# Bidirectional RWKV-7 flow step: the scans on 64-token blocks of two head pairs instead of 128-token chunks of one

## The reference

```python
def wkv_scan(s0, r, w, k, v, a, b, reverse):
    def step(S, inp):
        r_t, w_t, k_t, v_t, a_t, b_t = inp
        sa = jnp.einsum('bhvk,bhk->bhv', S, a_t)
        S = S * w_t[:, :, None, :] + sa[..., None] * b_t[:, :, None, :] + v_t[..., None] * k_t[:, :, None, :]
        return S, jnp.einsum('bhvk,bhk->bhv', S, r_t)
    s_final, y = lax.scan(step, s0.astype(jnp.float32), (...), reverse=reverse)
...
for d, (s0, reverse) in enumerate(((s0_f, False), (s0_b, True))):
    decay = jnp.exp(-jnp.exp(w_log.astype(jnp.float32)))
    y_d, s_d = wkv_scan(s0, r, decay, kd, v, -kk, kk * a, reverse)
wkv = ys[0] + ys[1]
mu = jnp.mean(wkv, axis=-1, keepdims=True)
var = jnp.mean(jnp.square(wkv - mu), axis=-1, keepdims=True)
ln = ((wkv - mu) * lax.rsqrt(var + LNX_EPS)).reshape(B, T, D_RWKV) * p['lnx_w'] + p['lnx_b']
x_a = (ln + (bonuses[0] + bonuses[1]).reshape(B, T, D_RWKV)).astype(xn.dtype) * g_out
```

## Time and profile before

| | us |
|---|---|
| median of 3 runs | 2689.25 (2687.86 to 2693.72) |
| span of the profiled execution | 2688.9 |
| dense stage, to 1008.5 us of the span | 1008.5 |
| scan stage, 1008.5 to 1625.5 | 617.0 |
| last stage, 1625.5 to the end | 1063.5 |
| TensorE busy over the whole span | 2568.6 (96%) |
| VectorE busy | 1872.8 (70%) |
| ScalarE, GpSimd busy | 1081.2 (40%), 1188.7 (44%) |

### The profile page before, as it was taken

The page is one execution under the profiler, slowest core; times in us unless marked ns, Lnnn a source line. Parts: engine busy times, 40 slices in busy tenths (PEclk is TensorE's granted clock), DMA queues, the critical chain, the costliest instruction groups (busy, mean ns, idle before and its releaser), DMA issues.

```text
span 2688.9 us, 67501 instructions
## 1 busy us (share of the span) xinstructions
PE 2568.6 (96%) x28608; PEld 2413.9 (90%) x28608; DVE 1872.8 (70%) x2978; ACT 1081.2 (40%) x1978; POOL 1188.7 (44%) x1154
## 2 busy tenths in 40 slices
PE   4899999999999998999999998999799999999998
PEld 3899999999999996777777777999799999999998
...
GB/s 325 106 102 118 140 71 186 113 111 140 80 175 123 101 203 116 131 133 149 142 155 139 145 162 181 133 179 98 61 63 86 81 101 63 87 82 100 63 79 71
DMA packets 282409, 329.10 MB, mean 122 GB/s; under 512 B 76288, under 2 KB 215936, under 8 KB 273536
## 3 DMA queue, kind: packets, MB, share of 16 engines
...
## 4 chain that ended last, share of the span: by engine, by line
PE 85%; DVE 8%; issue 2%; ACT 2%; DMA 2%; SPq 1%; POOL 0%; DVEq 0%; ACTq 0%; POOLq 0%
PE ser L972 18%; PE gbank L972 13%; PE inv L972 11%; PE bank L972 11%; PE gbank L1416 8%; PE inv L1416 8%; PE ser L1416 7%; PE bank L1416 7%; DVE a_sum L2323 1%; DMA ring<-in_wblocks 1%; PE inv L1174 1%; DVE a_sum L2327 1%; PE bank L1157 1%; DVE a_sum L2331 1%; DVE a_lo L2297 1%
## 5 line engine op out<-in xcount | busy, mean ns | idle before, releaser
L954 POOL TENSOR_TENSOR w_lo<-raw_w,w_hi 128x512 fp32r<-128x512 f32 x264 | 427.3, 1632 | 366.9 <-ACT w_hi L1756 366.9
L849 POOL TENSOR_TENSOR wsp<-ring,wsp 128x1024 fp32r<-128x1024 f32 x67 | 205.2, 3063 | 653.9 <-ACT wsp L1518 653.9
L1756 ACT ACTIVATE w_hi<-raw_w 128x512 fp32r<-128x512 f32 x264 | 165.2, 633 | 261.6 <-PE ser L1416 98.4
L972 PE MATMUL ser<-xn_hi,wsp 128*128 128x384 f32 x816 | 217.1, 339 | 6.0 <-POOL xn_lo L855 6.0
L1416 PE MATMUL gbank<-a_hi,w_hi 128*128 128x288 f32 x616 | 185.8, 302 | 30.8 <-POOL w_lo L954 14.6
L972 PE MATMUL gbank<-xn_hi,wsp 128*128 128x384 f32 x800 | 212.6, 339 | 0.3 <-issue 0.3
L972 PE MATMUL bank<-xn_hi,wsp 128*128 128x384 f32 x800 | 210.2, 337 | 0.5 <-issue 0.5
L972 PE MATMUL inv<-xn_hi,wsp 128*128 128x384 f32 x800 | 210.4, 338 | 0.0
L2126 DVE TENSOR_TENSOR gmat<-gbank,gmask 128x1024 f32<-128x1024 f32 x144 | 175.6, 1219 | 43.8 <-PE gbank L972 43.0
L1742 ACT ACTIVATE a_hi<-a_sum 128x1152 fp32r<-128x1152 f32 x88 | 103.0, 1172 | 224.5 <-DVE a_sum L2331 78.6
L972 PE MATMUL gbank<-ub 64*64 64x128 f32 (+1 forms) x3456 | 179.4, 310 | 9.0 <-DVE gmat L2126 7.6
...
## 6 DMA issues: line engine op xcount, KB each, us to landing
...
ub<-op_d SPq DMA_DIRECT2D x144, 256.0 KB, 2.8
...
```

The lines of the kernel that those rows point to most:

```text
L849: GT(wsp[s % 2][1][:], ring[(N_ADA_RING + s) % RING][:], wsp[s % 2][0][:].bitcast(F32), ALU.subtract).then_inc(S["wsplit_lo"], 1)
L954: GT(w_lo[n % 4][:], src, w_hi[n % 4][:].bitcast(F32), ALU.subtract).then_inc(S["wl_ok"], 1)
L972: return nc.tensor.matmul(out, lhsT, rhs, start=start, stop=stop)
L1756: A(w_hi[s][:], raw_of(op)[:, m, :].rearrange("p (k c) -> p k c", k=KH), ACT.Copy).then_inc(S["wh_ok"], 1)
```

## The change

A unit is now one block of 64 tokens of two head pairs (a group), both directions: 4 groups x 18 blocks = 72 units again. `LEVELS` goes from 6 to 5, so that the inverse ends at level 4 with two units in flight instead of three, and `last_blocks` on ACT is gone. `gmat` holds 64 columns per product instead of 128: half the elements. The 128 partitions of the token-side tensors, which were 128 tokens, are now 64 tokens of pair 0 and 64 tokens of pair 1. The second head's inverse, triangle and `ur` lie in the other partition half, which the index `b ^ h` says, so that the products of serial_ur, serial_u, serial_s and serial_y are 64*64 products. The state has one 64x64 tile per head pair, head and direction: 128x256 instead of two 128x64. It is now also carried over 18 blocks instead of 9 chunks. The loops of all engines are written in a new order (the lists below). DRAM scratch and loads follow the new tiling: one load of two units (7 DMAs) instead of 5 DMAs per unit; the `bk` planes are written in rows of 64 elements instead of 128. The dense stage scans 18 blocks of 64 tokens instead of 9 of 128. The finals stay one chunk of 128 tokens and one head pair: 18 per group, one per unit from block 10 of a group on, in the last group two per unit in units 64 to 71, with two left for the tail instead of five.

```diff
-LEVELS = 6
+LEVELS = 5
...
-UNITS = PAIRS * NC
-SETS = 5
-LOADS = 7
+
+GROUPS = PAIRS // 2
+UNITS = GROUPS * NB
+SETS = 4
+DOUBLES = 4
+PLACES = 2 * DOUBLES
 TOKS = 2
 LATE = LEVELS - FIRST
 FIN_ORDER = [3, 4, 2, 5, 1, 6, 0, 7, 8]
+FIN_FROM = 10
...
+        ar_d = scratch("ar_d", [GROUPS, 2, NC, P, 2, 2, C])
+        bk_d = scratch("bk_d", [GROUPS, 2, NB, P, 2, 2, HD])
+        v_d = scratch("v_d", [GROUPS, NC, P, 2, P])
...
+        def moving_of(v, d, b):
+
+            return ub[set_of(v)][:, d, b:4:2, tokens_of(d, v)]
+
+        def still_of(v, d, x):
+
+            return ub[set_of(v)][:, d, 4 + 2 * token_half(d, v) + x, :].rearrange("p (b t) -> p b t", b=2)
...
-            def start_inverse(v, part):
+            def start_inverse(v):
 
                 q, g = v % 3, gmat[v % SETS]
-                if part == 0:
-                    pool.wait_ge(S["gram_ok"], 2 * v + 2)
-                    for b in halves_of:
-                        ch.step(GT(ltc[q][b, :, :], g[b, 0, :, 0, b], g[b, 1, :, 0, b], ALU.add))
-                        ch.settle()
-                else:
-                    GT(lm[v % 2][part - 1][:], ltc[q][:], two(offm[:, part - 1, :]), ALU.mult).then_inc(S[f"lm{FIRST + part - 1}_ok"], 1)
+                pool.wait_ge(S["gram_ok"], 2 * v + 2)
+                ch.step(GT(ltc[q][:], g[:, 0, :, 0, :], g[:, 1, :, 0, :], ALU.add))
+                ch.settle()
+                for lev in range(FIRST, LEVELS):
+                    GT(lm[v % 2][lev - FIRST][:], ltc[q][:], two(offm[:, lev - FIRST, :]), ALU.mult).then_inc(S[f"lm{lev}_ok"], 1)
...
-                for n, b in enumerate(halves_of):
-                    for d in range(2):
-                        GT(tt[v % 2][b, d, :, b], xt[b, place_of(v), :, :], two(ttm[b, d, :]), ALU.mult).then_inc(S["tri_ok"], 1)
-                    pool.wait_ge(S["tri_ok"], 4 * v + 2 * n + 2)
+                pool.wait_ge(S["xt_ok"], sums(round_of(v)))
+                for d in range(2):
+                    GT(tt[v % 2][:, d, :, :], xt[:, place_of(v), :, :], two(ttm[:, d, :]), ALU.mult).then_inc(S["tri_ok"], 1)
...
+            def gram(v, d):
+
+                if d:
+                    pe.wait_ge(S["gram_ok"], 2 * v + 1)
+                else:
+                    pe.wait_ge(*loaded(v))
+                    if v:
+                        pe.wait_ge(S["gram_ok"], 2 * v)
+                for h in range(2):
+                    hs = halves_of[h]
+                    for b in range(2):
+                        mm(banks[h][halves_of[b ^ h], gram_at(d, 0, 1)], moving_of(v, d, b)[hs, 0, :], still_of(v, d, 0)[hs, b, :], True, True)
+                for h in range(2):
+                    hs = halves_of[h]
+                    for b in range(2):
+                        mm(banks[h][halves_of[b], gram_at(d, 1, 2)], still_of(v, d, 0)[hs, b, :], moving_of(v, d, b)[hs, 1, :], True, True)
+                for h in range(2):
+                    hs = halves_of[h]
+                    for b in range(2):
+                        ins = mm(banks[h][halves_of[b], gram_at(d, 2, 4)].rearrange("p (a t) -> p a t", a=2), still_of(v, d, 1)[hs, b, :], moving_of(v, d, b)[hs, :, :], True, True)
+                ins.then_inc(S["gram_full"], 1)
...
             def ur_state(u):
 
-                (p, j), q = divmod(u, NC), u % LOADS
-                serial_free(u)
-                if j < NC_LAT:
-                    pe.wait_ge(S["s_ok"], 2 * (NC_LAT * p + j + 1))
-                    for d in range(2):
-                        for h in range(2):
-                            hs = halves_of[h]
-                            for b in halves_of:
-                                mm(ser[b, h, d * HD:(d + 1) * HD], ub[q][hs, d, 0, b], state[d][j % 2][hs, :], d == 0, False)
-
-            def serial_ur(u):
-
-                j, q, g = u % NC, u % LOADS, gmat[u % SETS]
+                x = u % 2
                 for d in range(2):
                     for h in range(2):
-                        for b in halves_of:
-                            ins = mm(ser[b, h, d * HD:(d + 1) * HD], g[:, d, h, 2, b], vb[q][:, d, halves_of[h]], j == NC_LAT and d == 0, d == 1)
+                        hs = halves_of[h]
+                        for b in range(2):
+                            ins = mm(ser[halves_of[b ^ h], h, d * HD:(d + 1) * HD], moving_of(u, d, b)[hs, 0, :], state[x][hs, b, d, :], d == 0, False)
+                ins.then_inc(S["us_full"], 1)
+
+            def serial_ur(u):
+
+                q, g = set_of(u), gmat[u % SETS]
+                pe.wait_ge(S["us_full"], u + 1)
+                for d in range(2):
+                    for h in range(2):
+                        for b in range(2):
+                            bs = halves_of[b]
+                            ins = mm(ser[halves_of[b ^ h], h, d * HD:(d + 1) * HD], g[bs, d, h, 2, :], vb[q][bs, d, token_half(d, u), halves_of[h]], False, d == 1)
                 ins.then_inc(S["ur_full"], 1)
 
             def serial_u(u):
 
-                pe.wait_ge(S["tri_ok"], 4 * u + 4)
-                pe.wait_ge(S["tt_ok"], u + 1)
+                for x in finals(u - 1):
+                    pe.wait_ge(S["std_ok"], x[2] + 1)
+                pe.wait_ge(S["tri_ok"], 2 * u + 2)
                 pe.wait_ge(S["ur_ok"], u + 1)
                 for d in range(2):
                     for h in range(2):
-                        for b in halves_of:
-                            ins = mm(ser[b, 0, P + (2 * h + d) * HD:P + (2 * h + d + 1) * HD], tt[u % 2][:, d, h, b], ur[:, h, d, :], True, True)
+                        for b in range(2):
+                            xs = halves_of[b ^ h]
+                            ins = mm(ser[halves_of[b], h, P + d * HD:P + (d + 1) * HD], tt[u % 2][xs, d, h, :], ur[xs, h, d, :], True, True)
                 ins.then_inc(S["u_full"], 1)
 
             def y_at(j, d):
-                return slice((2 + y_place(d, j)) * P, (3 + y_place(d, j)) * P)
+                return slice(2 * P + y_place(d, j) * HD, 2 * P + (y_place(d, j) + 1) * HD)
 
             def y_state(u):
 
-                j, q = u % NC, u % LOADS
-                pe.wait_ge(S["ur_ok"], u + 1)
-                if j < NC_LAT:
-                    for d in range(2):
+                j, x = u % NB, u % 2
+                pe.wait_ge(S["xt_ok"], sums(round_of(u) + 1))
+                for d in range(2):
+                    for b in range(2):
                         for hs in halves_of:
-                            mm(ser[hs, 1, y_at(j, d)], state[d][j % 2][hs, :], ub[q][hs, d, 1, :], d == 0, False)
+                            ins = mm(inv[hs, b, y_at(j, d)], state[x][hs, b, d, :], moving_of(u, d, b)[hs, 1, :], d == 0, False)
+                ins.then_inc(S["ys_full"], 1)
...
-                    turn(s)
+            for s in range(-LATE - 1, UNITS):
+                m, j = divmod(s, NC)
+                inverses, serial, ahead = in_flight(s), there(s), there(s + 3)
+                if serial:
+                    serial_free(s)
+                    for x in finals(s - 1):
+                        variance(*x)
+                    ur_state(s)
                 if there(s + 1):
                     token_major(s + 1)
                 if serial:
-                    ur_state(s)
...
-            def last_blocks(v, n):
-
-                a, b = halves_of
-                at = slice(LATE * HD, (LATE + 1) * HD)
-                act.wait_ge(S["xt_ok"], sums(n + 1))
-                act.wait_ge(S["dt_full"], n + 1)
-                A(tt[v % 2][a, 0, :, b], inv[a, :, at], ACT.Copy)
-                A(tt[v % 2][b, 1, :, a], inv[b, :, at], ACT.Copy).then_inc(S["tt_ok"], 1)
...
-                for c in range(NC):
-                    o, x = (cum[:, c * C:(c + 1) * C], lw[:, c * C:(c + 1) * C])
+                for c in range(NB):
+                    o, x = (cum[:, c * HD:(c + 1) * HD], lw[:, c * HD:(c + 1) * HD])
                     if d == 1:
                         o, x = o[:, ::-1], x[:, ::-1]
-                    ch.step(V.tensor_tensor_scan(o, ones[:], x, 0.0, mul, add))
+                    ch.step(V.tensor_tensor_scan(o, ones[:, 0:HD], x, 0.0, mul, add))
...
                 dve.wait_ge(S["gram_full"], 2 * v + d + 1)
-                V.tensor_tensor(gmat[v % SETS][:, d, :, :, :].rearrange("p h x t -> p h (x t)"), gbank[:, :, :],
-                                gmask[:, d:d + 1, :].to_broadcast([P, 2, 4 * P]), mul).then_inc(S["gram_ok"], 1)
+                V.tensor_tensor(gmat[v % SETS][:, d, :, :, :].rearrange("p h x t -> p h (x t)"), gbank[:, :, 4 * d * HD:4 * (d + 1) * HD],
+                                gmask[:, d:d + 1, :].to_broadcast([P, 2, 4 * HD]), mul).then_inc(S["gram_ok"], 1)
...
+                dst = state[1 - u % 2] if j < NB - 1 else sfin
+                if j == NB - 1 and g:
+                    dve.wait_ge(S["sf_out"], 64 * g)
+                ch.step(V.tensor_tensor(dst[:], ser[:, :, 2 * P:3 * P].rearrange("p b (d v) -> p b d v", d=2), scale_of(u), mul))
```

(2 more changed lines are left out.)

690 lines of the change are left out of this document (337 added, 353 removed).

## The result

The changed kernel takes 2735.97 us (median of 5, 2733.36 to 2756.04), the kernel before, run beside it, 2688.58 (2685.68 to 2693.72): ratio 1.0188, 95% interval 1.0158 to 1.0219. It is slower by 47 us, where 31 us less was forecast (2658, in a range of 2628 to 2700). The profiled execution is the slowest of the five, with a span of 2754.2, so 18 us above the median; what follows on its stages is to be read with that in mind.

A forecast was written before the change was run, and what follows sets the result against it. The prediction took TensorE itself as the bound: rounds, changes of shape and three waits made 7.5 us a unit with finals; units, ramp, joints and tail made a scan stage of 585.5 us, 31 less, so 2658, range 2628 to 2700.

The forecast's parts named there:

- rounds: TensorE instructions that run together, four quarters or two halves of the array: 0.058 us for 64 columns, 0.109 for 128.
- changes of shape: TensorE's switches of tile shape between blocks: 0.14 us each, ten in a changed unit, 1.40 us.
- own time: TensorE's time in a unit with finals without waits for other engines: 5.98 us.
- rival D: Scan stage: TensorE less filled, its clock falls to half, 4.3 us more per unit at low clock; slower; chance 0.12.
- The three waits: TensorE in a unit: spread for the reciprocal 0.68 us, right for ScalarE's copy 0.66, y_state for the sum 0.23.
- the ramp: Start of the scan stage: 3 steps instead of 4 and shorter masks, about 12 us instead of 21.9.
- The other early units: Units 0 to 9, without finals: about 5.7 us each.
- Units 64 to 71: Last eight units, two chunks each, with VectorE's three operations twice and another spread and gate: 9.0 us each.
- Dense stage: 144 more scans, 23 us of VectorE's time, taken as 0 on the total, at most 10 if banks come late.
- B (shared banks): serial_ur and serial_u: two row halves writing one PSUM bank run one after the other, 0.47 us a unit, 2692; chance 0.08.
- C (VectorE late): Scan units: VectorE's list, about 4.9 us of 7.5, runs late, 0.4 us a unit more, 2683; chance 0.12.

The follow-up runs named there:

- run 7: Changed kernel with pairs of products for the two scan directions merged into one of 128 columns, 32 products a unit less, second direction's values wrong: 2685.99 us.
- run 2: Changed kernel with VectorE's reciprocal issued ahead of the gram mask instead of behind it: 2700.45 us.

## Why the prediction was wrong

**What bounds TensorE.** The prediction read "TensorE itself is the bound", and priced it by rounds, changes of shape and waits behind other engines. That held for the kernel before, and hid the next bound: at 5.2 us of issue waits and blocks of 256 instructions in 5 us, the list had little room left. Each of the changed blocks was priced by its columns alone, and the sum then took 7.5 us for a unit whose 452 instructions are 1.8 blocks of 256. This is the step that failed: waits for instructions and time at half clock stood at nothing in the sum. Measured, the issue waits are 30.9 us in the stage for 5.2 before, and the time at half clock 127 us for 21, by the two prices an estimated 31 to 36 us; beside them the unit's own time was 0.42 us too small. The trace of before had the sign, inside a block of TensorE near the end of its scan stage:

```profile
1598.55 0.45 PE L972 MATMUL ser<-state,ub 64*64 64x64 f32 x13 [0.20 <-DVE yf L2191]
1600.28 0.33 PE L972 MATMUL ser<-state,ub 64*64 64x64 f32 x3 [1.28 <-issue]
```

It stands at the same place of a 256 as the others, and right ahead of the fall of the clock (from 1601.28 on) from which rival D was argued.

**The unit.** Forecast 7.5, measured 7.92 where nothing disturbs it. The three waits were right by place, engine and size: 0.66 for 0.68 (`spread`), 0.74 for 0.66 between what `left` covers and `right` (0.50 of it shown as idle), 0.26 for 0.23 (`y_state`). The own time was too small: state to tokens is 0.39 where 4 rounds and a change are 0.37, tokens to `serial_ur` 0.58, `turn` to gram 0.36, gram 0.51 for 0.45; ten changes of shape at 0.15 to 0.18 in place of 0.14 and the gram make up most of the 0.4. Over 54 units that is 23 us, three quarters of the gain. Seven of the twelve units of 226 passes in the middle without an issue wait or a low clock take 7.92 us, so it is no single case.

**First and last units.** The first unit took 5.81 for 5.7 and the ramp 11.55 for 12, both right. The other early units should have been 5.7 too; the `ur` of the first ten start 68.2 us apart where 51 was forecast, since these densest units meet the issue waits first (one of 3.7 us among them); in run 7, which has nearly none, they are 57.2, so 6 us of the 17 would be there even so. Units 64 to 71 took 9.29 in the mean for 9.0.

**Dense stage.** The first gram is at 1014.07 for 1008.58: 5.5 us, inside the bound of 10. The scans cost VectorE 7 us, not 23 (busy in 100 to 1004 us 586.5 for 579.7).

**Rivals.** B (shared banks) is refuted: `serial_ur` takes 0.40 us to the next block where `ur_state` takes 0.39, and only the first has two row halves in one bank; the rule of the Trainium skill that the prediction cited for B (page "TensorEngine Tiling (Array Packing)", section "Gotcha 1: PSUM Pressure") is not borne out here. C (VectorE late) did not come. D named the right sign and a real mechanism, a granted clock under 0.95 (it was 0.91, one in five at half clock). It had the price too high, 4.3 us for a unit wholly at half clock where 0.29 us per us gives about 3.2, and its cause only half: run 7 keeps the waits that D blamed and gets 0.97, run 2 takes one of them away, keeps the issue waits, and gets 0.95. With D's one in five and the undisturbed unit of 7.92 the forecast would have been about 2715 (2658 + 23 + 122 x 0.29); the issue waits, 24 to 26 us, are about the remaining 20. Merging instructions brought 50 us, of which at least the 28 of issue waits hang on the instruction stream, and with them a part of the falls of the clock that can't be told apart from the part of D's waits.
